# A two-layer decoder step on one core: a new beginning with zero products, token rows written in three pieces, and eight transposes moved four units later

## The chip, the cores and the metric

One core of a Trainium2 chip runs the whole program once. The metric is the device time of that one execution in microseconds, the median over runs. TensorE (PE) multiplies, VectorE (DVE), ScalarE (ACT) and GpSimd (POOL) work element by element, and DMA queues, issued from SyncE (SP), ACT or POOL, move data between HBM and the on-chip memory.

## What is computed

264 tokens (256 of a prompt, 8 samples) with 1024 features go through two layers. Cut to what matters here:

```
h = h + mixer(rmsnorm(h, norm1[i]) @ w_in[i] ...) @ w_o[i]        # pooling + retention heads
hn = rmsnorm(h, norm2[i])
h = h + (swiglu(hn, ...) if i == 0 else moe(hn, ...))             # dense, then 8 experts, top 2
h = h + sigmoid(h @ w_ple_gate[i]) * (p[i] @ w_ple[i])
y = rmsnorm(h, final_norm)
# rmsnorm(x, g) = x * rsqrt(mean(x * x) + eps) * g
```

Everything is in 32-bit floats. The kernel keeps that accuracy by splitting each operand in a high part (rounded to the format `fp32r`) and a low part (the rest), and adding three products: high by high, low by high, high by low.

## The kernel before

`h` holds the 264 tokens as columns, in 8 chunks of 128 features. Weights come in units (128 x 2048 numbers in the mixer, 128 x 1408 or 128 x 1024 for the experts). SP loads them into a ring (`raw`), ACT makes the high part (`hi`, tile `whi`), DVE the low part in place (`lo`, tile `wlo`), and PE uses them. Each engine runs its own list of instructions in order, and the lists are tied by counting semaphores: `raw_landed`, `hi_ready`, `lo_ready`, and `unit_used`, which PE raises as it finishes a unit and which frees ring space for ACT and SP. The order is written out by hand; there is no planner.

**The start.** SP issues unit 0 of `w_in` (1 MB), the gains, `x` in two halves (0.5 MB each), a first piece of the constants, unit 1, and then the rest. ACT splits unit 0, then makes eight high parts `xh` (`part`), eight squares (`square`) and unit 1's high part. DVE makes the low parts. PE multiplies unit 0: its two outputs of 128 features one after the other, each of 8 row blocks `k` with three products of 264 columns. POOL adds the eight squares into `ssum`, one after the other, through two buffers `sq`. PE then takes the mean with one 32-bit product (`side_step(0, "norm1")`) between units 0 and 1. ACT takes the root, DVE the reciprocal `rstd`, and DVE scales the outputs of units 0 and 1 with it, which frees their banks for unit 2 and on.

**Expert 0 and the token rows.** Each expert has 16 gate and up units (`gate_up(e, i)`, nine products each) and 11 down units. Expert 0 and 1 take their tokens straight from `xth` and `xtl` on chip (`gather`). Later experts' tokens are gathered by DMA from a table `tokens` in HBM. For it POOL adds the two parts, `xt = xth + xtl`, in one instruction of 128 x 3072, once the last on-chip gather is done, and writes the three row blocks out. DVE at the same place computes the router's gates, starting with `dm`.

**The sum of six experts.** The outputs of experts 0 to 5 are added into a table `summed` in HBM by DMA. POOL reads it back into `xt` when expert 5's part has landed. PE transposes it for each of the 8 feature chunks (`summed_columns(m)`, three transposes), one chunk behind each of the units i = 7 to 14 of expert 7's gate and up. The first waits for `sum_in`. DVE adds each into `h` (`scattered`).

Of the kernel before, what the change touches and what calls it, by code (L numbers as in the profile page):

```python
# [25 lines left out]
F32 = mybir.dt.float32  # L26
F32R = mybir.dt.float32r
I32 = mybir.dt.int32
ALU = mybir.AluOpType
# [3 lines left out]
P = 128  # L33
# [285 lines left out]
SQUARES_AT = {0: 0, 1: 8, 3: 16, 4: 24, 6: 32}  # L319
GAIN = {0: 0, 1: 2, 3: 1}  # L320
NORM_STAGE = {(0, "norm1"): 0, (0, "norm2"): 1, (1, "norm1"): 3, (2, "norm1"): 6}
NORM_ORDER = {k: i for i, k in enumerate(NORM_STAGE)}

# [35 lines left out]
SCATTER_AFTER = 7  # L359
# [16 lines left out]
def program(nc, t):  # L376

    with ExitStack() as ctx:
# [34 lines left out]
        qk = place("qk", [P, 2, RC, T])  # L413
        wsum_at = at[0]
# [100 lines left out]
        x_in, first_in, const_in, layer_in = sem("x_in"), sem("first_in"), sem("const_in"), sem("layer_in")  # L515
# [55 lines left out]
        def h_final(eng, stage, m):  # L571

            if stage == 0:
                eng.wait_ge(x_in, 48)
# [13 lines left out]
        def unit_lo(u):  # L588

            return wlo[:, LOW_AT[u]:LOW_AT[u] + COLS[u]]  # L590

# [25 lines left out]
        def _(sp):  # L617
# [14 lines left out]

            def feed_forward():
# [32 lines left out]
            dense(0, U_MIX[0] + 2, W_IN[2:])  # L666
# [29 lines left out]
        def _(pe):  # L696
# [22 lines left out]
            def unit_pair(u, n, xhi, xlo, row_ready=None):  # L719

                pe.wait_ge(lo_ready, u + 1)
                chunk(n, n, u, DC, 256, 0, xhi, xlo, row_ready).then_inc(acc_full, 1)
                chunk(n + 1, n + 1, u, DC, 256, 1, xhi, xlo).then_inc(unit_used, 1)

# [53 lines left out]
            def side_step(l, name):  # L778
# [4 lines left out]
                if name in ("norm1", "norm2"):  # L783

                    pe.wait_ge(first_in, 16)
                    if l == DEPTH:
# [241 lines left out]
            def experts():  # L1028
# [6 lines left out]
                for kind, e in PHASES:  # L1035
                    for i in range(GU_UNITS if kind == "gu" else DOWN):
                        if kind == "gu":
# [25 lines left out]
                            if e == BY_DMA + 1 and 0 <= i - SCATTER_AFTER < DC:  # L1063
                                summed_columns(i - SCATTER_AFTER)
# [40 lines left out]

            for l in range(DEPTH):
                if l:
                    four_chunks(U_MIX[1], A_MIX[1], PARTS_AT[3], (1, "norm1"))
                for j in range(10):
                    if l == 0 or j > 1:  # L1110
                        unit_pair(U_MIX[l] + j, A_MIX[l] + 2 * j, xh, xl, (part_lo, PARTS_AT[0]) if l + j == 0 else None)
                    for name in AFTER[j]:
                        if (l, name) != (1, "norm1"):
                            side_step(l, name)
# [53 lines left out]
        def _(act):  # L1168
# [233 lines left out]
        def _(dve):  # L1402
# [341 lines left out]
            def experts():  # L1744
# [4 lines left out]
                for kind, e in PHASES:  # L1749
                    for i in range(GU_UNITS if kind == "gu" else DOWN):  # L1750
                        split_next(U_FF[1] + MOE_AT[kind, e] + i)
                        if kind == "gu":
# [13 lines left out]
                            if e == BY_DMA + 1 and 0 <= i - SCATTER_AFTER < DC:  # L1766
                                scattered(BY_DMA - 1, i - SCATTER_AFTER)
# [34 lines left out]
            lo(0)  # L1802
            for m in range(DC):
                finish(0, m)
            lo(1)
# [83 lines left out]
        def _(pool):  # L1889
# [65 lines left out]
            square_sum(0)  # L1955
# [133 lines left out]
```

## Time and profile before

| what | value |
|---|---|
| median of 3 runs | 968.57 us (968.2 to 971.69) |
| the profiled execution | 970.41 us, span of its trace 968.5 us |
| mean granted TensorE clock | 0.968 of full speed |
| PE busy | 908.9 us, 94% |
| DVE busy | 707.4 us, 73% |
| ACT busy | 523.1 us, 54% |
| POOL busy | 155.2 us, 16% |
| HBM | 241 GB/s over the span |

The span is what the trace covers; 1.9 us of the execution's time lie around it. The unit of a busy row is time in which at least one instruction of the engine ran; semaphore waits are not counted as busy.

### The profile page before, as it was taken

The numbers are of one execution on the slowest core, as the hardware profiler recorded it, in microseconds if no ns is written. First come the engines' busy times: TensorE is split into PE (matmuls) and PEld (weight loads), VectorE is DVE, ScalarE is ACT, GpSimd is POOL, SyncE is SP. The second block draws the span as 40 slices with busy tenths as digits, with TensorE's granted clock in tenths as the row PEclk, the third lists the DMA queues.
The fourth block names the chain that finished last, engine by engine and source line by source line (L and its number), as shares of the span: only waits on it lengthen the run. The fifth ranks groups of instructions, "written<-read, shape, count | busy, mean of one in ns | idle before, by whom it ended". The sixth has DMA issues, their size and how long they took to land.

```text
span 968.5 us, 14420 instructions
## 1 busy us (share of the span) xinstructions
PE 908.9 (94%) x5917; PEld 789.0 (81%) x5917; DVE 707.4 (73%) x829; ACT 523.1 (54%) x579; POOL 155.2 (16%) x178
## 2 busy tenths in 40 slices
PE   3999999999999997999988999999999999969976
PEld 3999799999999997999866777777777777747775
DVE  3786476655555675885568899888889898958955
ACT  5322364443445355222435778787878787837542
POOL 3336121100110013415213010001000100000001
PEclk9999999999999998999989999999999999989979
DMA  9973355746674656534236889999999999979601
GB/s 318 309 231 94 90 175 166 193 142 211 185 190 133 218 175 172 186 104 111 105 126 220 353 318 356 396 392 391 371 391 368 383 377 395 358 283 359 220 2 45
DMA packets 121827, 232.76 MB, mean 240 GB/s; under 512 B 5202, under 2 KB 89298, under 8 KB 121584
## 3 DMA queue, kind: packets, MB, share of 16 engines
q1 hardware_dynamic: 117664, 216.63, 63.1%
q0 software_dynamic: 4096, 15.19, 6.2%
q8 instruction: 48, 0.79, 0.4%
q14 instruction: 19, 0.16, 0.0%
HBM read 224.83 MB, written 8.52 MB: 241 GB/s over the span
## 4 chain that ended last, share of the span: by engine, by line
PE 80%; DVE 9%; ACT 5%; DMA 3%; issue 2%; POOL 1%; SPq 0%; DVEq 0%; ACTq 0%; POOLq 0%
PE bank L699 13%; PE bank L700 12%; PE bank L701 12%; PE bank L998 7%; PE bank L999 7%; PE bank L1000 7%; DVE wlo L1415 4%; PE bank L1024 4%; PE bank L1023 4%; PE bank L1025 4%; ACT whi L1175 2%; DMA xt<-summed 1%; DMA summed<-ys,to_row 1%; PE bank L857 1%; PE bank L865 1%
## 5 line engine op out<-in xcount | busy, mean ns | idle before, releaser
L1415 DVE TENSOR_TENSOR wlo<-raw,whi 128x1408 fp32r<-128x1408 f32 (+2 forms) x294 | 477.2, 1654 | 121.7 <-ACT whi L1175 121.5
L1175 ACT ACTIVATE whi<-raw 128x1408 fp32r<-128x1408 f32 (+2 forms) x294 | 398.1, 1381 | 189.9 <-PE bank L701 108.8
L699 PE MATMUL bank<-xh,whi 128*128 128x264 f32 x672 | 196.6, 293 | 18.8 <-DVE xl L1426 10.9
L700 PE MATMUL bank<-xl,whi 128*128 128x264 f32 x672 | 193.4, 288 | 0.0
L701 PE MATMUL bank<-xh,wlo 128*128 128x264 f32 x672 | 193.0, 287 | 0.0
L998 PE MATMUL bank<-whi,xeh 128*96 128x512 f32 (+1 forms) x384 | 145.9, 380 | 4.6 <-DVE wlo L1415 4.1
L699 PEld LDWEIGHTS bank<-xh,whi 128*128 128x128 f32 x672 | 129.7, 193 | 20.5 <-DVE wlo L1415 19.2
L999 PE MATMUL bank<-wlo,xeh 128*96 128x512 f32 (+1 forms) x384 | 145.0, 378 | 0.0
L1000 PE MATMUL bank<-whi,xel 128*96 128x512 f32 (+1 forms) x384 | 144.7, 377 | 0.0
L700 PEld LDWEIGHTS bank<-xl,whi 128*128 128x128 f32 x672 | 129.8, 193 | 0.4
L701 PEld LDWEIGHTS bank<-xh,wlo 128*128 128x128 f32 x672 | 129.1, 192 | 0.0
L998 PEld LDWEIGHTS bank<-whi,xeh 128*96 128x96 f32 x384 | 62.9, 164 | 25.8 <-DVE wlo L1415 5.3
L699 PE MATMUL bank<-mh,whi 128*128 128x264 f32 x256 | 75.7, 296 | 6.5 <-issue 5.5
L999 PEld LDWEIGHTS bank<-wlo,xeh 128*96 128x96 f32 x384 | 62.7, 163 | 19.7
L1000 PEld LDWEIGHTS bank<-whi,xel 128*96 128x96 f32 x384 | 62.4, 163 | 19.7
L700 PE MATMUL bank<-ml,whi 128*128 128x264 f32 x256 | 74.4, 290 | 0.0
L701 PE MATMUL bank<-mh,wlo 128*128 128x264 f32 x256 | 74.1, 290 | 0.0
L1023 PE MATMUL bank<-whi,hh 128*96 128x512 f32 x176 | 70.3, 400 | 0.0
L1024 PE MATMUL bank<-wlo,hh 128*96 128x512 f32 x176 | 69.3, 394 | 0.0
L1025 PE MATMUL bank<-whi,hl 128*96 128x512 f32 x176 | 68.9, 391 | 0.0
L699 PEld LDWEIGHTS bank<-mh,whi 128*128 128x128 f32 x256 | 50.1, 196 | 9.6 <-issue 7.7
L701 PE MATMUL bank<-fh,wlo 128*128 128x264 f32 x176 | 50.2, 285 | 0.0
(248 smaller groups left out, 1223.6 us busy)
## 6 DMA issues: line engine op xcount, KB each, us to landing
raw<-in_moe_w_gate SPq DMA_DIRECT2D x32, 1408.0 KB, 8.5
raw<-in_moe_w_up SPq DMA_DIRECT2D x32, 1408.0 KB, 9.1
raw<-in_moe_w_down SPq DMA_DIRECT2D x40, 1024.0 KB, 7.8
raw<-in_w_in SPq DMA_DIRECT2D x20, 1024.0 KB, 7.1
raw<-in_ffn_w_down SPq DMA_DIRECT2D x16, 704.0 KB, 5.0
raw<-in_ffn_w_gate SPq DMA_DIRECT2D x10, 1024.0 KB, 5.4
raw<-in_ffn_w_up SPq DMA_DIRECT2D x10, 1024.0 KB, 5.5
raw<-in_w_o SPq DMA_DIRECT2D x8, 1024.0 KB, 5.8
```

The source lines that it names most:

```text
L699: pe.matmul(out, w_hi, x_hi, start=start, stop=False)
L700: pe.matmul(out, w_hi, x_lo, start=False, stop=False)
L701: return pe.matmul(out, w_lo, x_hi, start=False, stop=stop)
L857: mm = pe.matmul(b[0:HD, a:a + 2], S[:, s, c, :], qm[:, s, c, :], start=True, stop=True)
L998: pe.matmul(b, X, H[:, lo:lo + n], start=(k == 0), stop=False)
L999: pe.matmul(b, X, L[:, lo:lo + n], start=False, stop=False)
L1000: mm = pe.matmul(b, Y, H[:, lo:lo + n], start=False, stop=(k == DC - 1))
L1023: pe.matmul(b, X, H[:, own], start=(i == 0), stop=False)
L1024: pe.matmul(b, X, L[:, own], start=False, stop=False)
L1025: mm = pe.matmul(b, Y, H[:, own], start=False, stop=(i == EC - 1))
L1175: act.activation(unit_hi(u), unit_raw(u), ACT.Copy).then_inc(hi_ready, 1)
L1415: dve.tensor_tensor(unit_lo(u), unit_raw(u), unit_hi(u).bitcast(F32), ALU.subtract).then_inc(lo_ready, 1)
```

## The change

Three things change; all arithmetic but the zero products is as before in result.

1. **The beginning.** `x` comes in four pieces of two chunks each, issued by ACT instead of SP, behind the gains. Unit 0 is loaded in two halves (row blocks 0 to 3 and 4 to 7), units 0 and 1 are split in halves by ACT and DVE. PE multiplies units 0 and 1 by row blocks, both outputs side by side (`first_pair`), and takes the mean between the halves of unit 1, not between units 0 and 1. The squares of chunks 0 to 4 are made by POOL and of 5 to 7 by ACT, POOL adds them in pairs, and PE sums the four pairs with four 32-bit products. Unit 2 is loaded ahead of the large constants. Ahead of everything PE multiplies a cleared tile by itself ten times, into a bank that nobody reads, and ACT runs one root of a single number.
2. **Token rows.** `xt` is added in three instructions of 128 x 1024, each behind units 8, 12 and 16 of expert 0, and each is written out at once.
3. **The sums.** The eight `summed_columns` stand in pairs behind units i = 11 to 14 instead of one behind each of 7 to 14.

```
-SQUARES_AT = {0: 0, 1: 8, 3: 16, 4: 24, 6: 32}
+SQUARES_AT = {1: 0, 3: 8, 4: 16, 6: 24}
-SCATTER_AFTER = 7
+SUM_AFTER = {11: (0, 1), 12: (2, 3), 13: (4, 5), 14: (6, 7)}
...
# SP
-            dense(0, U_MIX[0], W_IN[:1])
-            sp.dma_start(gains[:, :, :], t["gains"]).then_inc(x_in, 16)
-            sp.dma_start(h[:, 0:4, :], t["x"][:, 0:4, :]).then_inc(x_in, 16)
-            sp.dma_start(h[:, 4:8, :], t["x"][:, 4:8, :]).then_inc(x_in, 16)
+            first_rows(0, top_in)
+            first_rows(1, raw_landed[0])
             sp.dma_start(const[:, 0:FIRST_CONST], t["const"][:, 0:FIRST_CONST]).then_inc(first_in, 16)
-            dense(0, U_MIX[0] + 1, W_IN[1:2])
+            dense(0, U_MIX[0] + 1, W_IN[1:3])
...
# PE
+            def first_pair(u):
+                H = unit_hi(u).rearrange("p (k w) -> p k w", k=DC)
+                L = unit_lo(u).rearrange("p (k w) -> p k w", k=DC)
+                for half in range(2):
+                    pe.wait_ge(lo_ready if half else first_lo, u + 1)
+                    for k in range(4 * half, 4 * half + 4):
+                        if u == 0:
+                            pe.wait_ge(part_lo, k + 1)
+                        for m in range(2):
+                            own = slice(m * P, (m + 1) * P)
+                            mm = weights_first(bank[2 * u + m][:, 0:T], H[:, k, own], L[:, k, own], xh[:, k, :], xl[:, k, :],
+                                               k == 0, k == DC - 1)
...
+                    if u and half == 0:
+                        side_step(0, "norm1")
...
+                    if l + i == 0:
+                        for c in range(4):
+                            pe.wait_ge(first_sums, c + 1)
+                            mm = pe.matmul(b[:, 0:T], mean, first[:, 2 * c, :], start=(c == 0), stop=(c == 3))
...
-                            if e == BY_DMA + 1 and 0 <= i - SCATTER_AFTER < DC:
-                                summed_columns(i - SCATTER_AFTER)
+                            if e == BY_DMA + 1 and i in SUM_AFTER:
+                                for m in SUM_AFTER[i]:
+                                    summed_columns(m)
...
+            pe.wait_ge(still, 1)
+            for _ in range(10):
+                pe.matmul(bank[7][:, 0:T], sq[:, 0, 0:P], sq[:, 0, :], start=True, stop=True)
...
# ACT
-            hi(0)
-            h_final(act, 0, 0)
-            for m in range(DC):
-                part(0, m)
+            act.dma_start(gains[:, :, :], t["gains"]).then_inc(gains_in, 16)
+            for i in range(4):
+                act.dma_start(h[:, 2 * i:2 * i + 2, :], t["x"][:, 2 * i:2 * i + 2, :]).then_inc(x_in[i], 16)
+            act.wait_ge(still, 1)
+            act.activation(rstd[0:1, 0:1], sq[0:1, 0, 0:1], ACT.Sqrt)
+            hi_half(0, 0)
             for m in range(DC):
-                square(0, m)
-                if m == 2:
-                    hi(1)
+                h_final(act, 0, m)
+                part(0, m)
+                if m == 1:
+                    hi_half(0, 1)
+            for half in range(2):
+                hi_half(1, half)
+            for m in range(5, DC):
+                act.activation(first[:, m, :], h[:, m, :], ACT.Square).then_inc(first_sq, 1)
...
# POOL
-                pool.tensor_tensor(xt[:, :, :], xth[:, :, :].bitcast(F32), xtl[:, :, :].bitcast(F32), ALU.add).then_inc(xt_free, 1)
-                pool.wait_ge(xt_free, 1)
                 for j, w in BLK:
+                    pool.wait_ge(unit_used, U_FF[1] + 4 * (j + 2))
+                    pool.tensor_tensor(xt[:, j, :], xth[:, j, :].bitcast(F32), xtl[:, j, :].bitcast(F32), ALU.add).then_inc(xt_free, 1)
+                    pool.wait_ge(xt_free, j + 1)
                     pool.dma_start(tokens[j * P:j * P + w, :], xt[0:w, j, :]).then_inc(xt_out, 16)
...
-            square_sum(0)
+            pool.memset(sq[:, 0, :], 0.0).then_inc(still, 1)
+            for m in range(5):
+                pool.wait_ge(x_in[m // 2], 16)
+                pool.tensor_tensor(first[:, m, :], h[:, m, :], h[:, m, :], ALU.mult).then_inc(pool_step, 1)
+                steps += 1
+            pool.wait_ge(pool_step, steps)
+            for m in range(0, DC, 2):
+                if m >= 4:
+                    pool.wait_ge(first_sq, m // 2 * 2 - 3)
+                pool.tensor_tensor(first[:, m, :], first[:, m, :], first[:, m + 1, :], ALU.add).then_inc(first_sums, 1)
```

The order of ACT's first instructions, before (`whi` is a unit's high part, `xh` a chunk's, `sq` a square):

```order
L1175 ACTIVATE whi<-raw 128x2048 [waits raw_landed0]
L1185 ACTIVATE xh<-h,gains 128x264 [waits x_in]
L1185 ACTIVATE xh<-h,gains 128x264 x7
L1191 ACTIVATE sq<-h 128x264 x2
L1191 ACTIVATE sq<-h 128x264 [waits ss_added]
L1175 ACTIVATE whi<-raw 128x2048 [waits raw_landed1]
L1191 ACTIVATE sq<-h 128x264 [waits ss_added] x5
L1175 ACTIVATE whi<-raw 128x2048 [waits raw_landed2]
L1223 ACT_TABLE_LOAD [waits side_full]
```

And the same place of ACT after the change:

```order
L1364 DMA h<-in_x 128x528 x4
L1366 ACT_TABLE_LOAD
L1366 ACTIVATE rstd<-sq 1x1 [waits still]
L1359 ACTIVATE whi<-raw 128x1024 [waits top_in]
L1230 ACTIVATE xh<-h,gains 128x264 [waits x_in0,gains_in] x2
L1359 ACTIVATE whi<-raw 128x1024 [waits raw_landed0]
L1230 ACTIVATE xh<-h,gains 128x264 [waits x_in1,gains_in] x2
L1230 ACTIVATE xh<-h,gains 128x264 [waits x_in2,gains_in] x2
L1230 ACTIVATE xh<-h,gains 128x264 [waits x_in3,gains_in] x2
L1359 ACTIVATE whi<-raw 128x1024 [waits raw_landed1] x2
L1376 ACTIVATE first<-h 128x264 x3
L1220 ACTIVATE whi<-raw 128x2048 [waits raw_landed2]
```

The loading of ACT's table for the root has moved from behind the mean to the very front, and no square of ACT waits for POOL any more. On DVE the same place now reads, with halves of units (`wlo` 128x1024) between the low parts `xl` of the chunks:

```order
L1864 TENSOR_TENSOR wlo<-raw,whi 128x1024 [waits first_hi]
L1484 SCALAR_TENSOR_TENSOR xl<-h,gains,xh 128x264 [waits part_hi] x2
L1864 TENSOR_TENSOR wlo<-raw,whi 128x1024 [waits hi_ready]
L1484 SCALAR_TENSOR_TENSOR xl<-h,gains,xh 128x264 [waits part_hi] x6
L1864 TENSOR_TENSOR wlo<-raw,whi 128x1024 [waits first_hi]
L1864 TENSOR_TENSOR wlo<-raw,whi 128x1024 [waits hi_ready]
L1473 TENSOR_TENSOR wlo<-raw,whi 128x2048 [waits hi_ready]
L1524 RECIPROCAL rstd<-rstd 128x264 [waits std_ready]
```

Before, one split of 128 x 2048 stood ahead of all eight low parts and one behind them. On POOL, in expert 0, the list now reads as follows (`tokens` is the table in HBM, `xg` the gathered rows of experts 2 and 3):

```order
L2012 TENSOR_TENSOR xt<-xth,xtl 128x1024 [waits unit_used,ga_full]
L2014 DMA tokens<-xt 128x1024 [waits xt_free]
L2012 TENSOR_TENSOR xt<-xth,xtl 128x1024 [waits unit_used]
L2014 DMA tokens<-xt 128x1024 [waits xt_free]
L2012 TENSOR_TENSOR xt<-xth,xtl 128x1024 [waits unit_used]
L2014 DMA tokens<-xt 8x1024 [waits xt_free]
```

Before, one sum of 128x3072 that waited for `ga_full` alone stood ahead of the three writes.

## Rows read from the trace of the kernel before

**Rows 1.** Waits of PE, whole span: us in total, times, longest us
```profile
PE bank L943 <- DMA xt<-summed: 7.5, 1, 7.5
...
PE bank L998 <- DVE wlo L1415: 4.1, 1, 4.1
```

**Rows 2.** Timeline of the start: start us, length us, instruction, [idle before <-releaser]
```profile
5.94 1.91 ACT L1175 ACTIVATE whi<-raw 128x2048 fp32r<-128x2048 f32 x1 [3.90 <-DMA raw<-in_w_in]
...
9.67 3.36 ACT L1185 ACTIVATE xh<-h,gains 128x264 fp32r<-128x264 f32 x8 [1.82 <-DMA h<-in_x]
...
10.86 0.56 PE L699 MATMUL bank<-xh,whi 128*128 128x264 f32 x1 [10.86 <-DVE xl L1426]
...
18.48 0.28 PE L701 MATMUL bank<-xh,wlo 128*128 128x264 f32 x1
...
22.70 1.22 PE L795 MATMUL bank<-ssum,const 128*128 128x264 f32 x2 [3.94 <-POOL ssum L1906]
```

**Rows 3.** Timeline of ACT and DVE around the second and third unit
```profile
25.81 1.80 DVE L1466 RECIPROCAL rstd<-rstd 128x264 f32<-128x264 f32 x1 [0.45 <-ACT rstd L1223]
...
32.01 1.92 ACT L1175 ACTIVATE whi<-raw 128x2048 fp32r<-128x2048 f32 x1 [4.42 <-PE bank L701]
...
37.81 1.92 ACT L1175 ACTIVATE whi<-raw 128x2048 fp32r<-128x2048 f32 x1 [3.88 <-PE bank L701]
```

**Rows 4.** Stretches: us, busy of PE, PEld, DVE, ACT, POOL; PEclk, DMA share, GB/s
```profile
5.00:10.00 5.00, 0.00 (x0) 0.00 (x0) 2.12 (x1) 2.24 (x2) 0.00 (x0) 1.00 1.03 363
...
25.00:30.00 5.00, 5.00 (x30) 5.00 (x29) 4.52 (x5) 2.57 (x3) 3.80 (x9) 0.64 1.10 323
```

**Rows 5.** Timeline at units 8 to 18 of the experts, and one chain piece
```profile
520.29 7.92 POOL L1942 TENSOR_TENSOR xt<-xth,xtl 128x3072 f32<-128x3072 f32 x1 [22.43 <-PE bank L920]
...
521.91 6.32 DVE L1644 TENSOR_TENSOR dm<-m,m 128x3 f32<-128x3 f32 x1
...
530.17 9.30 DVE L1415 TENSOR_TENSOR wlo<-raw,whi 128x1408 fp32r<-128x1408 f32 x6
...
531.84 0.74 PE L998 MATMUL bank<-whi,xeh 128*96 128x512 f32 x1 [4.06 <-DVE wlo L1415]
...
538.38 0.44 PE bank L951 x6
...
540.79 3.35 DVE L1415 TENSOR_TENSOR wlo<-raw,whi 128x1408 fp32r<-128x1408 f32 x2
...
555.02 0.44 PE L998 MATMUL bank<-whi,xeh 128*96 128x512 f32 x1 [0.57 <-DVE hid L1721]
```

**Rows 6.** Timeline around expert 7's unit 7, ACT and PE
```profile
852.09 1.38 ACT L1175 ACTIVATE whi<-raw 128x1408 fp32r<-128x1408 f32 x1 [0.52 <-PE bank L1000]
...
853.99 1.38 ACT L1175 ACTIVATE whi<-raw 128x1408 fp32r<-128x1408 f32 x1 [0.53 <-PE bank L1000]
...
861.38 0.89 PE L943 MATMUL bank<-const,xt 128*128 128x128 f32 x3 [7.48 <-DMA xt<-summed]
...
865.67 1.38 ACT L1175 ACTIVATE whi<-raw 128x1408 fp32r<-128x1408 f32 x1 [10.30 <-PE bank L1000]
...
868.14 1.38 ACT L1175 ACTIVATE whi<-raw 128x1408 fp32r<-128x1408 f32 x1 [1.08 <-PE bank L1000]
```

**Rows 7.** Single durations elsewhere: half-width splits, one POOL sum, eight chain pieces
```profile
575.86 1.06 ACT L1175 ACTIVATE whi<-raw 128x1024 fp32r<-128x1024 f32 x1 [1.04 <-PE bank L1000]
...
578.86 1.23 DVE L1415 TENSOR_TENSOR wlo<-raw,whi 128x1024 fp32r<-128x1024 f32 x1 [0.39 <-ACT whi L1175]
...
88.58 0.64 POOL L2004 TENSOR_TENSOR wsum<-upad 128x271 f32<-128x271 f32 x1
...
37.71 1.78 PE bank L800 x8
```

**Rows 8.** The first gather of token rows, and the products that take it
```profile
576.42 2.92 POOL L1928 DMA_INDIRECT xg<-tokens,from_row  x1 [46.30 <-issue]
...
586.46 0.52 PE bank L929 x4
```

More of the change, by code:

```diff
@@ L318 @@
 PARTS_AT = {0: 0, 1: 8, 2: 16, 3: 24, 5: 32}
-SQUARES_AT = {0: 0, 1: 8, 3: 16, 4: 24, 6: 32}
+SQUARES_AT = {1: 0, 3: 8, 4: 16, 6: 24}
 GAIN = {0: 0, 1: 2, 3: 1}
-NORM_STAGE = {(0, "norm1"): 0, (0, "norm2"): 1, (1, "norm1"): 3, (2, "norm1"): 6}
-NORM_ORDER = {k: i for i, k in enumerate(NORM_STAGE)}
+NORM_STAGE = {(0, "norm2"): 1, (1, "norm1"): 3, (2, "norm1"): 6}
+NORM_ORDER = {(0, "norm1"): 0} | {k: i + 1 for i, k in enumerate(NORM_STAGE)}
 AFTER = [["norm1"], [], [f"rq{c}" for c in range(RC)], [], [f"rk{c}" for c in range(RC)],
@@ L413, in program @@
         qk = place("qk", [P, 2, RC, T])
+        first = place("first", [P, DC, T], F32, arena)
         wsum_at = at[0]
@@ L513, in program @@
         hi_ready, lo_ready, unit_used = sem("hi_ready"), sem("lo_ready"), sem("unit_used")
-        x_in, first_in, const_in, layer_in = sem("x_in"), sem("first_in"), sem("const_in"), sem("layer_in")
+        x_in, gains_in, top_in = [sem(f"x_in{i}") for i in range(4)], sem("gains_in"), sem("top_in")
+        first_in, const_in, layer_in = sem("first_in"), sem("const_in"), sem("layer_in")
+        first_hi, first_lo, first_sq, first_sums = sem("first_hi"), sem("first_lo"), sem("first_sq"), sem("first_sums")
+        still = sem("still")
         pool_kept, state_out, y_out = sem("pool_kept"), sem("state_out"), sem("y_out")
@@ L573, in h_final @@
             if stage == 0:
-                eng.wait_ge(x_in, 48)
+                eng.wait_ge(gains_in, 16)
+                eng.wait_ge(x_in[m // 2], 16)
             else:
@@ L590, in unit_lo, with unit_half @@
             return wlo[:, LOW_AT[u]:LOW_AT[u] + COLS[u]]
+        def unit_half(x, u, half, at=LOW_AT):
+            n = COLS[u] // 2
+            return x[:, at[u] + half * n:at[u] + (half + 1) * n]
         def unit_hi(u):
@@ L631, in dense, with first_rows @@
                     load(u, m[k0 * P:(k0 + n) * P, c0:c0 + w], n, w)
+            def first_rows(half, landed):
+                name, _, n, c0, w = W_IN[0]
+                n //= 2
+                dst = unit_half(raw, 0, half).rearrange("p (k w) -> p k w", k=n)
+                src = t[name][0][half * n * P:(half + 1) * n * P, c0:c0 + w]
+                sp.dma_start(dst, src.rearrange("(k p) w -> p k w", p=P)).then_inc(landed, 16)
             def feed_forward():
@@ L1109, in _ @@
                 for j in range(10):
-                    if l == 0 or j > 1:
-                        unit_pair(U_MIX[l] + j, A_MIX[l] + 2 * j, xh, xl, (part_lo, PARTS_AT[0]) if l + j == 0 else None)
+                    if j > 1:
+                        unit_pair(U_MIX[l] + j, A_MIX[l] + 2 * j, xh, xl)
+                    elif l == 0:
+                        first_pair(j)
                     for name in AFTER[j]:
-                        if (l, name) != (1, "norm1"):
+                        if name != "norm1":
                             side_step(l, name)
@@ L1309, in experts, with hi_half @@
                                 y_out_hi(e)
-            hi(0)
-            h_final(act, 0, 0)
+            def hi_half(u, half):
+                act.wait_ge(raw_landed[LANDING[u]] if u or half else top_in, 16)
+                act.activation(unit_half(whi, u, half, HIGH_AT), unit_half(raw, u, half),
+                               ACT.Copy).then_inc(hi_ready if half else first_hi, 1)
+            act.dma_start(gains[:, :, :], t["gains"]).then_inc(gains_in, 16)
[4 more added lines that the diff above has]
+            hi_half(0, 0)
             for m in range(DC):
+                h_final(act, 0, m)
                 part(0, m)
-            for m in range(DC):
-                square(0, m)
-                if m == 2:
-                    hi(1)
+                if m == 1:
[4 more added lines that the diff above has]
+                act.activation(first[:, m, :], h[:, m, :], ACT.Square).then_inc(first_sq, 1)
             for l in range(DEPTH):
@@ L1765, in experts @@
                                 slot_values((e + 1) // 2, bank[6])
-                            if e == BY_DMA + 1 and 0 <= i - SCATTER_AFTER < DC:
-                                scattered(BY_DMA - 1, i - SCATTER_AFTER)
+                            if e == BY_DMA + 1 and i in SUM_AFTER:
+                                for m in SUM_AFTER[i]:
+                                    scattered(BY_DMA - 1, m)
                             if i == GU_UNITS - 1:
@@ L1800, in over_expert, with lo_half @@
                     dve.tensor_tensor(h[:, m, :], h[:, m, :], osg[:, :], ALU.add).then_inc(o_done, 1)
-            lo(0)
+            def lo_half(u, half):
+                dve.wait_ge(hi_ready if half else first_hi, u + 1)
+                dve.tensor_tensor(unit_half(wlo, u, half), unit_half(raw, u, half), unit_half(whi, u, half, HIGH_AT).bitcast(F32),
+                                  ALU.subtract).then_inc(lo_ready if half else first_lo, 1)
+            lo_half(0, 0)
             for m in range(DC):
                 finish(0, m)
-            lo(1)
+                if m == 1:
+                    lo_half(0, 1)
+            for half in range(2):
+                lo_half(1, half)
             for l in range(DEPTH):
```

6 lines of the change are left out of this document (4 added, 2 removed).

## The prediction

> **What bounds the kernel now.** I read the waits of PE first, because PE is busy for 94% of the span: whatever keeps it from working is on the path. Three places stand out. Two are in the list [rows 1]: 7.5 us before the transposes of the summed rows, and 4.1 us in expert 0. The third is the start, read in the timeline [rows 2]. PE's first product is at 10.86, behind ACT's split of unit 0 (begun at 5.94, when it landed) and `xh` (begun at 9.67, when `x` landed). Unit 0 ends at 18.48 + 0.28, and PE idles until 22.70, released by POOL's sum of squares. ACT's next split, which waits for unit 1 to be used, starts at 32.01 and the next at 37.81 [rows 3]: 5.80 us is a full-speed unit of 48 products, 0.121 us each, so unit 1 (from 23.3) took some 2.9 us too long. The stretch 25 to 30 says why: a granted clock of 0.64, so partly the 1.2 GHz level, after that idle time [rows 4]. From 32 on PE is busy without a hole, so what the start saves shifts all that follows.
>
> In expert 0 [rows 5], POOL's 128 x 3072 sum runs from 520.29 to 528.21, and DVE's `dm`, three numbers wide, takes 6.32 us and ends at 528.23. The six low parts behind it start at 530.17, and PE, which wanted unit 8 at 527.78, gets it at 531.84. In expert 7 [rows 6] ACT's releases come 1.90 us apart (852.09, 853.99), then 11.68 later (865.67), then 2.47 (868.14, a unit with three transposes). The transposes begin at 861.38, when the rows have landed.
>
> **The change, part by part.** Times are on the clock of the trace before.
>
> *The start.* Unit 0 is 1.05 MB and landed at 5.94; the queue moves 363 GB/s [rows 4]. Half of it, alone, would land 1.4 us earlier, at 4.5; if the pieces of `x` from ACT's queue take every second byte, at 5.9 again. I take 5.8, because the descriptors of `x` are the longer ones. The second half and all of `x` are the same 2.1 MB as before, whose end was 9.67; I take 8.4 for the half.
>
> The Trainium skill (DMA: Bandwidth & Descriptors, "Issuing engines are not separate DMA queues") says that DMAs of several issuing engines run on the same 16 engines and interleave, and that a second issuer saves only issue time. If it were wrong and the second queue brought its own rate, the half would land at 4.5 and the start would be worth some 1.3 us more.
>
> A half-width split is 1.06 us on ACT and 1.23 on DVE, and one POOL sum of this size 0.64 [rows 7]. ACT: 5.8 + 1.06 = 6.9. DVE: + 1.23 = 8.1. POOL's squares 2 to 4 fall due just then; [rows 5] show that while POOL reads two tensors DVE's two-tensor work stands still. I put one of them, 0.7, in DVE's way, and 0.4 for the first `xl` (3.36 us for the eight `xh` beside it gives the same pitch): PE starts at 9.2, not 10.86. The second half: ACT 8.4 to 9.5, DVE behind another POOL instruction 10.2 to 11.4, `xl` of chunk 2 at 11.9. From there DVE needs 0.42 per chunk and PE 6 x 0.121 = 0.73, so PE sets the pace: six chunks, 16.2. Unit 1's first half, 24 products: 19.1. The mean is now four 32-bit products on PE where one was; eight chain pieces, four such products, are 1.78 us [rows 7]: 20.9. The squares are through by then (ACT's three at 15.3, POOL's last pair near 17.3). Second half: 23.8. The root (0.5) and reciprocal (1.80, [rows 3]) end at 23.2, the first scaling at 23.6, so unit 2 does not wait. Unit 1 is used at 23.8 instead of 31.95: **8.1 us**.
>
> The zero products hide the slow clock: a 32-bit product is 1.78 / 4 = 0.45 us at full speed, so ten are 4.5, and 8.9 at half; begun near 1.1 (an estimate), they end near 8 if the clock rises on the way, and the holes of about a microsecond behind them are shorter than any that lowered it in these rows. Bounds for the start: 9.5 (nothing of POOL in the way), 5 (half lands at 7, POOL's last pair waits behind a full split, half clock to 13).
>
> *Token rows.* PE loses 4.06 us at unit 8 and works at half clock behind it. From 531.84 to 555.02 it does ten units (19.05), the slot values (6 small products, 0.44; 0.5 with what hangs on it) and a wait of 0.57 for `hid`: 3.0 us too much. Without POOL's big sum `dm` is done at 522.1, unit 8's low part starts 1.94 later as before (528.23 to 530.17), at 524.0, and PE does not stop there. But the same 6.3 us of standing still come back, one third behind each of units 8, 12 and 16, while DVE is the fuller engine here. Its work from 524.0 to `hid`: twelve low parts of 1.55 (9.30 for six) 18.6, slot values 1.32 (539.47 to 540.79), POOL's three pieces 6.3: 550.2, and 0.7 for the first `hid`: 550.9. PE would be there at 527.78 + 19.05 + 0.5 = 547.3 and waits. So unit 18 starts at 551 instead of 555.02: 4.1, and I take **3.8 us**, since a hole of 3.6 us may cost a little clock. Bounds: 7.2 (the pieces fall where DVE waits anyway), 0.5 (the pieces take 2.6 each as the big one's length says, and the hole brings half clock for some 4 us).
>
> This is the rule that speaks against spreading the sum. The Trainium skill (SBUF — State Buffer, "SBUF: two separate sides") calls the port pair that DVE and GpSimd share an exclusive lock held for a whole instruction, the loser being fully blocked. By it the blocked total does not shrink with smaller pieces; the trace agrees (`dm` ends within 0.02 us of POOL's sum).
>
> *The sums.* Four units of 1.90 more stand ahead of the first transpose: PE reaches it at 853.90 + 7.60 = 861.5, and the rows landed at 861.38. The whole excess of that step is 11.68 - 2.47 = 9.2 us (7.48 idle, the rest half clock). I take **8.9**, with 0.3 of wait left. The transposes themselves stay, two sets behind one unit; DVE then has 0.86 for `h` and 1.23 for a split in 3.0 us. Bounds: 9.2, and 6 if the rows land 3 us later because weights are now loaded without a pause.
>
> *Sum.* 8.1 + 3.8 + 8.9 = 20.8. The profiled execution took 970.41 (span 968.5 and 1.9 around it): 949.6. It lay 1.84 above the median of the three; on that median the forecast is 947.8, say **948**.
>
> **The rivals.**
> - *Forecast*, each term near its value, 945 to 951.5: 0.64.
> - *DVE does not recover in expert 0.* POOL's pieces push `hid` so late that the gain there is nothing: 948 + 3.8, about 952. For it: DVE is full from 530 to 555. Against: from 544.1 to `hid` near 554 it had only four more low parts to make, 6.2 us of work in 10. 0.13.
> - *The pieces cost nothing*, because they fall in DVE's waits for ACT: 948 - 3.4, about 944.5. 0.12.
> - *The sums' wait survives.* The read back of the rows shares the queues with weights that no longer pause; landing 3 us later leaves 3 us of wait: 951. For it: the weight loads that wait for PE now go on beside it. Against: the ring's free room was filled beside it before, too. 0.05.
> - *The zero products do not raise the clock, or the halves land late*: unit 0 at half speed for 4 us and a later start, 951. The place to look is the spacing of the first real products. 0.04.
> - *Slower: the token table is late.* The gather of rows for expert 2 was issued at 576.42 and its products began at 586.46 [rows 8]. It now waits for three pieces, the last behind unit 16. If DVE's back-to-back splits kept POOL from the port, the piece would end late. By plan it ends near 548; from about 16 us later PE waits for the gather, and only past 16 + 21 = 37 us, at 585, is all the gain gone. At 590, 973 us. Against: POOL's big sum got in between two splits. 0.01.
> - *The change does not do what it says* (holes stay where they were), 968: 0.01.
>
> **How the numbers follow.** 948 is the likeliest case. The cases from 943 to 954 hold a little over 8 in 10, the sum of the bad bounds (5 + 0.5 + 6 = 11.5, so 957) and of the good ones (25.9, so 943) mark the ends. A measurement of this kernel can tell 0.5%, 4.8 us, from no change. Faster by more than that: 0.97; within it: 0.02; slower: 0.01.
>
> **What the profile of the changed kernel would show.** First real product near 9.2, spaced 0.12 within a block; no hole between units 0 and 1; ACT's split that waits for unit 1 at 23.8. `dm` 0.2 us long; three POOL sums of 2.1 us; DVE splits of 3 to 4 us beside them; a PE wait for `hid` of 3 us at unit 18. The wait for the summed rows under 1 us. I would be wrong if the first product came after 11, if PE waited for low parts in several places of expert 0, or if the transposes still waited for over 3 us.

## The result

The changed kernel takes 955.03 us (median of 4, 953.66 to 957.95), the kernel before in the same comparison 969.47 (968.2 to 971.69). The ratio is 0.9853, 95% interval 0.9821 to 0.9885: 14.3 us faster, not the 20.8 of the forecast, and one microsecond outside the 943 to 954 that were to hold 8 cases in 10. The profiled execution took 957.95, the slowest of the four; its span is 956.2 at a mean clock of 0.974.

The start, timeline of the kernel after (columns as in [rows 2]):

```profile
1.12 6.95 PE L1148 MATMUL bank<-sq 128*128 128x264 f32 x20 [1.12 <-POOL sq L2024]
...
8.74 0.36 PE L715 MATMUL bank<-xh,whi 128*128 128x264 f32 x1 [0.67 <-DVE xl L1484]
...
19.57 1.94 PE L824 MATMUL bank<-first,const 128*128 128x264 f32 x8
21.16 0.48 PE L715 MATMUL bank<-xh,whi 128*128 128x264 f32 x1
...
24.54 0.36 PE L715 MATMUL bank<-xh,whi 128*128 128x264 f32 x1
...
40.79 0.36 PE L715 MATMUL bank<-xh,whi 128*128 128x264 f32 x1 [2.63 <-DVE qk L1624]
```

Up to 24.5 the start went as forecast: first product 8.74 (9.2 said), the mean at 19.57 (19.1), the second half of unit 1 at 21.16 (20.9), unit 1 used near 24 instead of 31.95. Then PE stands still for 2.63 us at 40.79. Why, ACT, DVE and POOL show, the same kernel:

```profile
18.50 1.90 POOL L2037 DMA_DIRECT2D S<-in_state_ret  x1
...
22.86 0.55 POOL L2043 DMA_DIRECT2D out_new_pool_sample<-in_state_pool  x1
...
24.29 1.91 ACT L1220 ACTIVATE whi<-raw 128x2048 fp32r<-128x2048 f32 x1 [2.19 <-DMA raw<-in_w_in]
...
36.06 1.92 ACT L1220 ACTIVATE whi<-raw 128x2048 fp32r<-128x2048 f32 x1 [9.86 <-DMA raw<-in_w_in]
...
38.01 2.29 DVE L1473 TENSOR_TENSOR wlo<-raw,whi 128x2048 fp32r<-128x2048 f32 x1 [8.80 <-ACT whi L1220]
...
39.53 1.91 ACT L1220 ACTIVATE whi<-raw 128x2048 fp32r<-128x2048 f32 x1 [1.56 <-DMA raw<-in_w_in]
...
40.22 0.76 DVE L1624 SCALAR_TENSOR_TENSOR qk<-bank,rstd 128x264 f32<-128x264 f32 x2
...
42.55 1.92 ACT L1220 ACTIVATE whi<-raw 128x2048 fp32r<-128x2048 f32 x1 [1.11 <-DMA raw<-in_w_in]
46.94 1.91 ACT L1220 ACTIVATE whi<-raw 128x2048 fp32r<-128x2048 f32 x1 [2.46 <-PE bank L717]
```

The four splits of units 3 to 6 wait for weights to land, unit 4 for 9.86 us. DVE's low part of unit 4 waits for that split, and `qk`, which frees the bank that PE wants, stands behind the low part in DVE's list. In [rows 3] the splits at this place waited for PE. Meanwhile POOL has issued six transfers for layer 0 (states, pooling weights, `p`: 2.3 MB by their sizes). Before, it issued the same six 4 us later, as the timeline of that kernel shows:

```profile
22.50 1.89 POOL L1959 DMA_DIRECT2D S<-in_state_ret  x1
```

Stretches of the kernel after (columns as in [rows 4]):

```profile
25.00:30.00 5.00, 5.00 (x44) 5.00 (x43) 2.97 (x3) 1.20 (x1) 0.00 (x0) 1.00 1.06 236
...
39.00:42.00 3.00, 1.21 (x10) 1.24 (x11) 2.96 (x6) 1.91 (x1) 0.00 (x0) 1.00 1.09 349
```

From 25 to 30 the DMA engines are full (1.06) and move 236 GB/s, not the 349 of the second row. (In the kernel before, [rows 4] have a share of 1.10 and 323 GB/s in this stretch.)

Waits of PE, kernel after, without the two longest, which have their like before (9.5 and 5.3 us in sum, against 8.5 and 5.5; columns as in [rows 1]):

```profile
PE bank L715 <- DVE qk L1624: 2.6, 1, 2.6
PE bank L968 <- DMA xg<-tokens,from_row: 2.6, 2, 1.6
...
PE bank L880 <- DVE vpad L1542: 1.6, 1, 1.6
...
PE bank L1037 <- DVE wlo L1473: 0.7, 1, 0.7
PE bank L1037 <- DVE hid L1779: 0.5, 1, 0.5
```

The 7.5 and 4.1 of [rows 1] are gone. New are the first three of these lines. The first is the wait at 40.79. The second is for token rows fetched for experts 2 to 5, which arrive late, 1.6 and 1.0 us. The third stands at 65.81, for `vpad`, behind a row of DVE that has had no pause since its late low part at 38.01:

```profile
65.81 0.46 PE L880 MATMUL bank<-sc,vpad 128*128 128x128 f32 x2 [1.56 <-DVE vpad L1542]
```

Expert 0, timeline of the kernel after, to be laid beside [rows 5]:

```profile
522.86 0.15 DVE L1702 TENSOR_TENSOR dm<-m,m 128x3 f32<-128x3 f32 x1
...
524.95 11.51 DVE L1473 TENSOR_TENSOR wlo<-raw,whi 128x1408 fp32r<-128x1408 f32 x6
...
528.02 5.38 DVE L1473 TENSOR_TENSOR wlo<-raw,whi 128x1408 fp32r<-128x1408 f32 x2
...
528.88 3.03 POOL L2012 TENSOR_TENSOR xt<-xth,xtl 128x1024 f32<-128x1024 f32 x1 [30.05 <-PE bank L1039]
...
537.13 2.49 POOL L2012 TENSOR_TENSOR xt<-xth,xtl 128x1024 f32<-128x1024 f32 x1 [4.34 <-PE bank L1039]
537.46 2.19 DVE L1759 SCALAR_TENSOR_TENSOR empty<-rgs,spare 96x2 f32<-96x2 f32 x1
...
545.67 5.70 POOL L2012 TENSOR_TENSOR xt<-xth,xtl 128x1024 f32<-128x1024 f32 x1 [5.17 <-PE bank L1039]
...
549.04 1.92 DVE L1779 SCALAR_TENSOR_TENSOR hid<-bank,rgs,hid 96x512 f32<-96x512 f32 x3
...
549.92 0.44 PE L1037 MATMUL bank<-whi,xeh 128*96 128x512 f32 x1 [0.53 <-DVE hid L1779]
```

The first piece gets in between the third and the fourth of six splits and adds 2.2 us to them (11.51 against 9.30; the two around it take 5.38, where two in a row took 3.15 before). The second adds 2.0 to `empty` (0.16 before). The third waits from 545.67 and ends at 551.37, beside `hid`, which takes the same 1.92 us as before: it costs DVE nothing ahead of unit 18, and some 0.4 in the split behind `hid` (1.97 against 1.61). `dm` stood 0.95 later here than before, unit 18 starts 5.10 earlier (549.92 against 555.02): this stretch gained 6.05 us.

The sums, timeline of the kernel after around expert 7's units 10 to 14:

```profile
854.78 1.38 ACT L1220 ACTIVATE whi<-raw 128x1408 fp32r<-128x1408 f32 x1 [0.52 <-PE bank L1039]
...
856.69 1.38 ACT L1220 ACTIVATE whi<-raw 128x1408 fp32r<-128x1408 f32 x1 [0.52 <-PE bank L1039]
...
858.34 1.06 PE L982 MATMUL bank<-const,xt 128*128 128x128 f32 x6
...
861.32 1.05 PE L982 MATMUL bank<-const,xt 128*128 128x128 f32 x6
```

The releases come every 1.90 us up to the transposes, and no wait for the summed rows is left.

### The profile page after: what moved, and what is told of

Read it like the earlier page. It is cut to its first block, busy times and chain, and to the rows that moved or that the text cites. A ratio compares the mean times of both kernels' runs of the same rounds, so it can differ in the third digit from the quotient of the medians.

```text
span 956.2 us, 14481 instructions
## 1 busy us (share of the span) xinstructions
PE 911.9 (95%) x5943; PEld 791.2 (83%) x5943; DVE 707.7 (74%) x831; ACT 521.1 (54%) x576; POOL 163.1 (17%) x182
## 4 chain that ended last, share of the span: by engine, by line
PE 73%; DVE 13%; DMA 4%; issue 4%; ACT 4%; SPq 2%; DVEq 0%; ACTq 0%; POOLq 0%
PE bank L715 12%; PE bank L716 11%; PE bank L717 11%; DVE wlo L1473 7%; PE bank L1037 6%; PE bank L1038 6%; PE bank L1039 6%; PE bank L1063 4%; PE bank L1062 4%; PE bank L1064 4%; DMA xg<-tokens,from_row 2%; DMA raw<-in_w_in 2%; ACT whi L1220 2%; PE bank L896 1%; PE bank L904 1%
## 5 line engine op out<-in xcount | busy, mean ns | idle before, releaser
L1037 PE MATMUL bank<-whi,xeh 128*96 128x512 f32 (+1 forms) x384 | 143.8, 374 | 1.2 <-DVE wlo L1473 0.7
L1039 PEld LDWEIGHTS bank<-whi,xel 128*96 128x96 f32 x384 | 61.7, 161 | 19.1
```

The lines of the kernel that those rows point to most:

```text
L1037: pe.matmul(b, X, H[:, lo:lo + n], start=(k == 0), stop=False)
L1039: mm = pe.matmul(b, Y, H[:, lo:lo + n], start=False, stop=(k == DC - 1))
```

## The experiments

Every kernel was compared with the kernel before on its own chip; medians are of 4 to 12 executions; "gain" is one minus the ratio, times that chip's median of before (970.6 to 971.0 us). The first table lists the parts, each alone and two together:

| kernel | median | ratio, 95% interval | gain, us |
|---|---|---|---|
| start_only | 968.9 | 0.9975 (0.9962 to 0.9989) | 2.4 |
| tokens_only | 964.52 | 0.9938 (0.9918 to 0.9959) | 6.0 |
| sums_only | 960.86 | 0.9896 (0.9882 to 0.9911) | 10.1 |
| old_start (tokens and sums) | 954.14 | 0.983 (0.9817 to 0.9842) | 16.5 |
| after_again (all three) | 955.6 | 0.985 (0.9835 to 0.9865) | 14.6 |

**start_only** is the kernel after with these lines of before:

```
+SCATTER_AFTER = 7    # in place of SUM_AFTER, on PE and DVE
+                pool.tensor_tensor(xt[:, :, :], xth[:, :, :].bitcast(F32), xtl[:, :, :].bitcast(F32), ALU.add).then_inc(xt_free, 1)
+                pool.wait_ge(xt_free, 1)
                 for j, w in BLK:
-                    pool.wait_ge(unit_used, U_FF[1] + 4 * (j + 2))
-                    pool.tensor_tensor(xt[:, j, :], ...)
```

> The kernel before with the new beginning alone. Theory A (the profile after: unit 1 is used 8.1 us earlier, but units 3 to 6 land late, DVE is full from 51 to 66, and the clock falls earlier around 96 and 143, so that the second norm of layer 0 comes 1.1 us later than before): 968 to 971 us, no change. Rival B (the start is worth its 8.1 us and the shortfall belongs to the other two moves): 961 us. In the profile, A wants the split that waits for unit 4 to land near 36 and the second norm near 149; B wants it near 140.

It gave 2.4 us (1.1 to 3.7), close to A and far from B. In its profile unit 4's split starts at 35.48, as A wanted, but the second norm (`rstd`) at 145.77, between A's 149 and B's 140. So most of the missing microseconds belong to the start.

**tokens_only** is the kernel before with the last two lines put in and the big sum taken out.

> The kernel before with the token rows in three pieces alone. By the landmarks of the profile after, the stretch from the router to expert 0's unit 18 is 4.7 us shorter, of which the gathers of rows, now waited for twice, take about 1.7 back by expert 7: 965 to 966 us. If the pieces cost nothing the stretch would be 7.2 us shorter: 962. If DVE does not recover in expert 0: 969.

6.0 us (4.0 to 8.0), more than my 3.8, and near the 6.05 that the stretch of expert 0 gained in the profile of after. **sums_only** is the kernel before with `SUM_AFTER`.

> The kernel before with the eight summed columns behind units 11 to 14 alone. Theory (the whole step of 11.68 us falls back to 2.4): 9.0 to 9.3 us less, 960 us. Rival (weights loaded without a pause hold the rows back by 3 us): 963 us. PE waits for the summed rows under 0.5 us by the theory, 3 us by the rival.

The theory held: PE's list has no wait for the summed rows, and 10.1 us (8.6 to 11.5) holds the whole step of 9.2 in its interval; from expert 0's `dm` to the last `rstd` its profile is 9.45 us shorter than before.

**old_start** is both together on the kernel before.

> The kernel before with the pieces of the token rows and the moved sums, and with the old beginning. The two moves alone gave 6.4 and 10.1 us. If they add up (the beginning is then what does not add, worth nothing beside them): 954 us. If they take from each other (the fetches of rows): 956 to 957, and the beginning is then worth the same 1 to 2 us with them as without them.

They add up: 16.5 against 16.1. And without the new beginning the kernel is as fast as with it, or faster.

### What takes the start's gain

**loads_held** issues POOL's six transfers of layer 0 behind the four rotations of q:

```
 for l in range(DEPTH):
-    pool.dma_start(S[:, :, :, :], ...)      # and five more
+    if l:
+        layer_loads(l)
...
     for a, name in enumerate(("rq", "rk")):
         for c in range(RC):
             pool.wait_ge(side_full, SIDE[l, f"{name}{c}"] + 1)
             pool.tensor_tensor(qk[:, a, c, :], qk[:, a, c, :], C("cos"), ALU.mult).then_inc(cosed, 1)
+        if l + a == 0:
+            layer_loads(0)
```

> The kernel after, with POOL's six transfers of layer 0 (2.3 MB: states, pooling weights, rows of p and the copy of the pooling state) issued behind the four rotations of q instead of at the start; POOL's memsets stay ahead. Theory A (these transfers share the DMA engines with units 3 to 6 and make them late): unit 4 lands 4 to 7 us earlier than 36.1, the wait of 2.6 us near 41 goes, and the time is 2.5 to 4 us less than the kernel after, 951 to 952.5; all 8.1 us do not come back, since DVE is full from 51 to 66. Rival C (units 3 and 4 are late because the large constants stand ahead of them on SP's queue, whatever POOL loads): unit 4 lands at 34 or later and the time stays at 955. Rival D (the states arrive after POOL wants to multiply them at 53): slower than the kernel after, 957 or more.

951.01 us, ratio 0.9811 (0.9788 to 0.9833). Its timeline and one stretch, at the place shown above:

```profile
26.90 1.92 ACT L1220 ACTIVATE whi<-raw 128x2048 fp32r<-128x2048 f32 x1 [2.16 <-DMA raw<-in_w_in]
30.56 1.92 ACT L1220 ACTIVATE whi<-raw 128x2048 fp32r<-128x2048 f32 x1 [1.74 <-PE bank L717]
```

```profile
25.00:30.00 5.00, 5.00 (x44) 5.00 (x43) 3.89 (x4) 1.92 (x1) 0.00 (x0) 1.00 1.09 348
```

Unit 4 lands 9.2 us earlier than in the profile of after (more than A's 4 to 7; in after_again, the same kernel, its split starts at 34.46, so 7.6 there), from unit 5 on ACT waits for PE again, and the DMA engines, as full as before, move 348 GB/s instead of 236. Theory A holds, C and D fall. The next two set the beginning and the transfers against each other on the kernel before (same edit):

> The kernel before, with POOL's six transfers of layer 0 issued behind the four rotations of q and nothing else. Theory A (the transfers cost time only where PE would otherwise run ahead of the weights; in the kernel before PE is the slower of the two from unit 3 on, no wait for weights stands in its list): 0 to 1.5 us less than before, 969.5 to 971. Rival E (the transfers cost some 5 us in any kernel, by contention that does not show as a wait): 966.

> The kernel before with the new beginning and with the same six transfers held back. Theory A (new beginning and held transfers are worth together what neither is alone: 8.1 us less the 1.3 us by which the profiled execution of before was slow in the stretch 25 to 30): 963 to 965 us against 968.9 for the new beginning alone and some 970.5 for the held transfers alone. Rival F (the clock takes back what is saved, whatever the loads do): 968. In its profile the split of unit 4 starts near 27 and that of unit 7 at 44, against 46.4 with the transfers at the start.

| | transfers at the start | held back |
|---|---|---|
| old beginning | 1 | 1.0005 (0.9994 to 1.0015) |
| new beginning | 0.9975 (0.9962 to 0.9989) | 0.9938 (0.9924 to 0.9953) |

Held transfers are worth nothing alone, and raise the value of the new beginning from 2.4 to 6.0 us. Rivals E and F fall. **states_held** holds back one of the six, the 1 MB of retention states:

```
-                pool.dma_start(S[:, :, :, :], ...)
+                if l:
+                    pool.dma_start(S[:, :, :, :], ...)      # for layer 0 behind the rotations of q
```

> The kernel after with the transfer of the retention states alone (1 MB of the 2.3, in rows of 256 bytes) held back behind the rotations of q. If bytes count alone, it is worth half of what all six are (4.4 us): 953. If its small rows are what crowds the weights: nearly all, 951.5. If the order of the queue behind it counts and not its bytes: 955.

950.17 us, 0.9793 (0.9779 to 0.9807): all of the time and not half. In its timeline unit 4's split starts at 31.31, and two units later ACT waits for PE; two stretches follow:

```profile
31.31 1.92 ACT L1220 ACTIVATE whi<-raw 128x2048 fp32r<-128x2048 f32 x1 [5.78 <-DMA raw<-in_w_in]
34.32 1.92 ACT L1220 ACTIVATE whi<-raw 128x2048 fp32r<-128x2048 f32 x1 [1.09 <-DMA raw<-in_w_in]
38.34 1.92 ACT L1220 ACTIVATE whi<-raw 128x2048 fp32r<-128x2048 f32 x1 [2.10 <-PE bank L717]
```

```profile
20.00:25.00 5.00, 4.90 (x35) 4.49 (x34) 3.11 (x4) 1.88 (x2) 2.96 (x8) 1.00 1.10 286
25.00:30.00 5.00, 5.00 (x43) 5.00 (x43) 2.98 (x3) 0.52 (x1) 0.00 (x0) 1.00 1.05 311
```

That is half the bytes and half of the 9.2 us of landing, but PE only needed unit 4 by then: what is left of the delay is in its shadow. The small rows of the states (256 bytes by the kernel's shapes) are not shown to be worse than the rest. The five other transfers are issued earlier here, so the dip begins earlier; over 20 to 35 the DMA engines move 315 GB/s on average, against 287 in the kernel after (344, 236, 281) and 348 in loads_held. The five bring 1.27 of the 2.32 MB, 55%, and 33 of the 61 GB/s of loss, 54%: the loss goes with the bytes. What is not in proportion is what PE makes of it.

### The zero products

**held_no_zeros** is loads_held without the ten products.

> The kernel after with held transfers and without the ten products of zeros. Theory (they keep the clock at its upper level at the first real product): the first units run at half clock for some 4 us, spacing 0.24 and not 0.12, which costs 1.5 to 3 us against 951.0: 952.5 to 954. Rival (DVE's low parts set the pace of unit 0 anyway, and the mean and its chain come later too): no difference, 951.

950.59 us, 0.979 (0.9777 to 0.9803): no loss, as the rival said. In its timeline the first products do run at half pace, and the stretch with them has a granted clock of 1.00:

```profile
8.36 0.56 PE L715 MATMUL bank<-xh,whi 128*128 128x264 f32 x1 [8.36 <-DVE xl L1482]
8.72 0.42 PE L716 MATMUL bank<-xl,whi 128*128 128x264 f32 x1
8.94 0.42 PE L717 MATMUL bank<-xh,wlo 128*128 128x264 f32 x1
```

```profile
8.00:9.00 1.00, 0.64 (x3) 0.67 (x4) 0.98 (x2) 1.00 (x2) 1.00 (x2) 1.00 1.05 374
```

0.22 us each (264 columns at 1.2 GHz), against 0.12 in the kernel after (2.4 GHz), and still so at 12.87; at 13.75 they are at 0.12. But loads_held, at full speed, then waits 1.3 us at 11.6 for the second half's low parts, and DVE sets the pace of the rest. The slow products fill a hole that is there anyway.

### POOL's pieces

**third_earlier** is the kernel after with `pool.wait_ge(unit_used, U_FF[1] + (8, 12, 14)[j])`.

> The kernel after with the third piece of the token rows behind unit 14 instead of 16 of expert 0. In the profile after the third piece began to wait at 545.67 and ended at 551.37, beside the three instructions of hid, which read a bank and were no longer than before: it cost DVE nothing. If POOL gets in only where DVE waits or reads a bank (Theory K), the piece ends at 551 again and the time is the same, 955.5. If it gets in at the next border between two splits (Rival L), it ends near 545 and blocks 2 us of DVE's row, and PE waits some 2 us longer for hid: 957.

955.77 us, 0.9859 (0.9829 to 0.989), the time of the kernel after, but this interval is too wide to tell K's 955.5 from L's 957. The timeline of DVE and POOL decides:

```profile
534.08 9.28 DVE L1473 TENSOR_TENSOR wlo<-raw,whi 128x1408 fp32r<-128x1408 f32 x6
543.29 1.91 DVE L1779 SCALAR_TENSOR_TENSOR hid<-bank,rgs,hid 96x512 f32<-96x512 f32 x3
...
535.15 10.46 POOL L2012 TENSOR_TENSOR xt<-xth,xtl 128x1024 f32<-128x1024 f32 x1 [0.40 <-PE bank L1039]
```

Asked for two units sooner, the piece stays out through six back-to-back splits and ends at 545.61, with `hid` (this profile is 5.7 us ahead of that of after here). For the third piece L falls. But K does not hold as a rule: the first piece, here as in every profile of a kernel with pieces, got in at the next border between two back-to-back splits (in the kernel after at 529.6, the rows at 528.02 and 528.88), with no wait of DVE and no bank read. Why one piece gets in there and the other does not, no run shows.

### The fetched rows, and best versions

The parts alone add to 18.5 us, all three give 14.6. **after_again** is the kernel after unchanged.

> The kernel after unchanged, on the same chip as the three others. The three moves alone gave 2.1, 6.4 and 10.1 us, together 18.6, where all three gave 14.4. If the moves do not add up (Theory G: rows of tokens are fetched in the shadow of weight loads with no slack, and each move shifts which fetch is late), it stays at 955 to 956.5; if the difference was chance of the draws (Theory H), 952 to 953.5. The wait for fetched rows in its profile was 2.6 us in sum, none in the kernel before.

It stays at 955.6, so Theory H, chance of the draws, falls. PE's wait for fetched rows was a candidate, although it is 0.7 us in this profile and 2.6 in that of after. **fetch_earlier** (on loads_held), **after_fetch** (on the kernel after), **old_start_fetch** and **states_fetch** share one edit:

```
-RG_AFTER = 10
+RG_AFTER = 8
```

> The kernel after with held transfers, and with the slot values of a later pair of experts taken two units earlier (behind unit 8, not 10), so that POOL issues the fetches of token rows some 3.8 us earlier. Theory G (the fetches have no slack: PE asks for the second one 8 to 11 us after its issue and waited for it 0.7 to 2.6 us in the profiles with the new beginning): no wait for fetched rows is left, 1 to 2.5 us less than 951.0, 948.5 to 950. Rival (the waits are draws of single executions, or the rows come late because weights are ahead of them whenever they are asked for): 951.

> The kernel after with fetches of token rows issued two units earlier. Theory G (late fetches are what the new beginning loses in company): 953, 2 to 2.5 us less than after. Rival: 955.5, no change.

> The old beginning with pieces and moved sums, and fetches two units earlier. In its profile there was no wait for fetched rows, so by Theory G nothing changes: 954, and the new beginning (after_fetch) is then 1 to 2 us better, as it was alone. By its rival the earlier fetches help here as much as there, or neither, and the beginnings stay equal.

> The kernel after with the retention states held back and fetches two units earlier: if both add, 950.2 less 2, 948 to 948.5; if the fetches bring nothing, 950.

**x_from_sp** issues the gains and `x` from SP:

```
-            act.dma_start(gains...)                  # and x in four pieces
+            sp.dma_start(gains...), x[0:2]
             first_rows(0, top_in)
+            sp.dma_start(x[2:4])
             first_rows(1, raw_landed[0])
+            sp.dma_start(x[4:6]), sp.dma_start(x[6:8])
```

> The kernel after with the gains and the pieces of x issued by SP between the halves of unit 0, and not by ACT. If the late fetches have to do with the queue that ACT issues on (Theory M): rows land 9.8 us after issue again, 1 to 2 us less than after, 953.5 to 954.5. If not, the fetches stay near 11 and only the start can differ: SP needs some 0.6 us for each issue, so the last quarter of x is issued some 2 us later than by ACT, and the time is 955 to 957.

| kernel | median | ratio, 95% interval | PE's wait for fetched rows, us |
|---|---|---|---|
| fetch_earlier | 949.06 | 0.9782 (0.9766 to 0.9798) | 0.5 |
| after_fetch | 953.98 | 0.9832 (0.9815 to 0.9849) | 1.5 |
| old_start_fetch | 955.09 | 0.9841 (0.982 to 0.9861) | none |
| states_fetch | 949.84 | 0.9794 (0.9768 to 0.982) | 0.5 |
| x_from_sp | 955.29 | 0.9849 (0.9828 to 0.987) | none |

In x_from_sp the rows landed 9.9 us after issue and PE never waited for them, yet it takes the time of the kernel after: Theory M, right on the landing, is wrong on the time. This alone does not clear the late rows, because its beginning is later too (`qxi` at 69.12, against 66.8 to 68.5 in the profiles that share the kernel after's). By the ratios the earlier fetches changed the time by -1.7 us on the kernel after, +1.1 on old_start, -2.8 on loads_held and +0.1 on states_held: both signs, and only the -2.8 lies just outside what its two intervals allow (2.7). No gain is shown, and so late rows are not shown to be where the difference went. The five kernels with all three moves and held transfers or states lie between 949 and 951 us, 4.6 to 6.5 below the kernel after; fetch_earlier's 949.06 is the lowest median, and which of them is best isn't settled.

## Why the prediction was wrong

*The step that failed* is the start's: "From 32 on PE is busy without a hole, so what the start saves shifts all that follows." The term was 8.1 us, its bounds 5 to 9.5; alone it measured 2.4 (1.1 to 3.7). Everything I costed up to unit 1 came within 0.5 us. What I did not ask was whether the weights of units 3 to 6 could follow a PE that is 8 us ahead. The answer stood in [rows 4]: a DMA share of 1.10 at 323 GB/s in the stretch 25 to 30. The DMA engines were full there; PE was merely late enough not to wait. How little room there was, tokens_only shows: with the old beginning, PE 1.3 us ahead at 71, its split of unit 5 waited for weights until 38.37.

To size the pieces I laid two landmarks of DVE side by side in the profiles: `qxi` (71.12 before) and the reciprocal of the second norm (149.07 before). Times relative to before:

| profiles | at 71 | at 149 |
|---|---|---|
| old beginning (6, before's 0 among them) | -1.0 (0 to -1.5) | +0.5 (-0.9 to +1.1) |
| new beginning (6) | -3.4 (-2.0 to -4.3) | -1.9 (-4.6 to +1.1) |
| new, six transfers or states held (6) | -7.0 (-6.7 to -7.3) | -5.1 (-3.3 to -7.3) |

Of the 8.1 us, 1.0 was before's own draw (a slower stretch at 25 to 30 than the other five), 3.7 is what the transfers take, shown by the table of four above, and 2.4 remain. The last 1 us fits weights that are late without POOL's transfers too (unit 4 at 26.90 where PE had room for it near 24); no run shows it by itself.

*Clock draws.* The profile of after had lost even the 2.65 us that it was ahead at 71. Stretches of the kernel after, and of start_only, which runs the same code here:

```profile
96.00:110.00 14.00, 12.76 (x85) 10.44 (x84) 6.48 (x19) 4.11 (x10) 2.19 (x4) 0.63 0.52 135
143.00:149.00 6.00, 3.86 (x19) 3.86 (x20) 4.29 (x2) 1.56 (x1) 0.00 (x0) 0.72 0.00 0
```

```profile
96.00:110.00 14.00, 12.60 (x95) 9.77 (x95) 7.05 (x19) 5.37 (x11) 2.85 (x4) 0.88 0.49 127
143.00:149.00 6.00, 6.00 (x51) 5.93 (x49) 3.81 (x4) 2.12 (x3) 0.00 (x0) 1.00 0.00 0
```

The granted clock behind the 64 tiny products of the states and behind the second norm's idle time is 0.63 and 0.72 in the one, 0.88 and 1.00 in the other; of the four kernels that differ from before only after 500 us, three had 0.76 and 0.72, and one 0.88 and 1.00, as before's own profile. Such draws move a landmark by up to 4 us, and my base, one profiled execution, held both a good and a bad one.

*Token rows.* Mechanism right, size off: 3.8 forecast, 6.0 (4.0 to 8.0) measured alone. DVE's row was right up to the third piece, which I let cost 2.1 us and which costs nothing ahead of unit 18; and the wait of 3 us for `hid` became 0.53.

*Sums.* Right: 8.9 forecast, 10.1 (8.6 to 11.5) measured, 9.45 by the landmarks, no wait left where I kept 0.3.

*Zero products.* I gave "they do not raise the clock" 951. They do raise it, and with held transfers it is worth nothing: a wrong reason that did not touch the sum.

*Luck.* The total missed by 6.2 us where its parts missed by 9.6 one way: the start gave 5.7 us less than forecast and all three together 3.9 less than their sum, while token rows and sums gave 3.4 more (2.2 and 1.2), which the forecast did not earn.

*What stays open* is that the new beginning, worth 2.4 us alone, is worth -1.9 (ratios 0.983 and 0.985) beside the other two moves, and +0.9 beside them with earlier fetches. The first two intervals, 1.1 to 3.7 and -3.8 to 0, do not quite meet, so this may be more than chance; no mechanism for a loss in company was found. A part of it, in the two profiles, looks like a clock draw far behind all three moves: at the last transposes of the sums after_again is still 0.8 us ahead of old_start, at the end 1.2 behind, and the turn falls in one stretch of 12 us in which the granted clock was 0.77 in after_again (915 to 927), 0.91 in old_start (916 to 928) and 0.91 in x_from_sp (918 to 930), which has the new beginning. The rivals did not contain the outcome: none said that a later resource takes the start's gain.

The rule cited on several issuing engines (the Trainium skill, DMA: Bandwidth & Descriptors, "Issuing engines are not separate DMA queues") was on the right side twice: `x` from SP or ACT makes no difference in time that these runs can tell, and POOL's transfers did take from SP's weights. I had used it for `x` and not for them.

## What to carry to other kernels

Before you credit a shift of the start to the end, find the first resource behind it that is already full although nobody waits for it: with a DMA share of 1 and no DMA wait in the list, work out whether the loads could follow an earlier consumer. Ask of every transfer on another queue whether it must be issued now; holding back 1 MB that nobody read for 20 us after it had landed (issued at 18.50, landed 12.7 us later, read by POOL at 53.24) gave more than the rewritten beginning had given by itself. Take the base of a forecast from the clock rows of several executions where the work is small and the clock falls, since a single one may be off by 4 us at a landmark.

## What the runs showed of the hardware that I had not expected

- A POOL sum of two tensors runs beside DVE instructions that read a bank and one tensor (`hid` 1.92 us with it and without), and once it stayed out through six back-to-back DVE splits of two tensors: 10.46 us for some 2.1 us of work (a third of `dm`'s 6.3). The first piece got in between two such splits and made them 2.2 us longer. The Trainium skill (SBUF — State Buffer, "SBUF: two separate sides") names as DVE's side of the lock an instruction with two inputs in SBUF, which fits `hid`; I had not applied it.
- Six transfers from POOL's queue, 2.3 MB beside the weights, lower what full DMA engines move from 348 to 236 GB/s for 5 us; without the 1 MB of states among them the mean over 20 to 35 us is 315 instead of 287 GB/s. A unit of weights behind them landed 7.6 to 9.2 us later.
- PE's first products after 8 us of idling ran at the 1.2 GHz level while the column of the granted clock said 1.00; only their spacing (0.22 against 0.12 us) shows it.
